# Attention of layer 0: scores in two passes from high and low parts, output written in parts, another order of units and modulation panels

## The chip, the core and the metric

The kernel runs on one core of a Trainium2 chip. The metric is the device time of one execution, in microseconds (us). Everything is fp32 data; the core's engines are TensorE (PE in the profile, matmuls), VectorE (DVE), ScalarE (ACT), GpSimd (POOL) and SyncE (SP, which issues most DMAs).

## The reference

Two transformer-like blocks of two layers each, on 512 tokens of width 1024 (and 256 context tokens in the first block). The change touches layer 0 of the first block, whose mixer is this:

```python
q, k, v = project(h)                        # 16 query heads, 4 key/value heads of 64
q, k = rope_2d(q, rows, cols), rope_2d(k, rows, cols)
qc, kc, vc = project(hc)                    # the same for the 256 context tokens
# tokens in 4 blocks of 128; each sees its own block, its neighbours (|distance| <= 128)
# and all 256 context tokens; a learned sink logit joins the softmax
s_win = einsum('bnqhgd,bnkhd->bnhgqk', qb, kw) * scale, masked
s_ctx = einsum('bnqhgd,blhd->bnhgql', qb, kc) * scale
p = softmax(concatenate([s_win, s_ctx, sinks]))
o = einsum(p_win, vw) + einsum(p_ctx, vc)
y = o.reshape(B, S, D_MODEL) @ w_o
# the context's own queries see only the 256 context tokens
```

Before and beside it, six modulation vectors (shifts, scales, gates) are made per layer by silu(c) @ ada_w + ada_b. A residual add, an MLP and then layer 1 and the second block follow; the change leaves them as they are.

## The kernel before

Every weight comes as a 1 MB "panel" (`sp_panels`, three buffers in a ring, issued by SP in the fixed order of `PANELS`). A projection is done to nearly fp32 accuracy from fp32r matmuls: `act_hi` (ScalarE) rounds a panel's half to fp32r, the high part, `dve_lo` (VectorE) subtracts to get the low part, the activations are split the same way, and `pe_tile` adds three matmuls per 128 rows of depth: high by high, low by high, high by low. Other matmuls take plain fp32 operands; the profile shows each of those as two records.

Each engine runs a program written out by hand, and its order is the order of the work. They meet only at semaphores (`wait_ge`, `then_inc`). Around the change the programs are, in time: modulation panels 0 to 7 and the first norm (`ada0_*`), queries, keys and values (`qkv_*`), attention (`att_*`), output projection (`wo_*` with the class `Proj`), MLP.

Attention works in 24 units: one group g (4 query heads that share a key head, 64 partitions) by one block of 128 queries. `AUNITS` lists them: 16 main units (query blocks 0 to 3, four groups each), then 8 context units. A main unit has 4 key blocks (query blocks 0 and 3) or 5 (1 and 2), a context unit 2. For unit n:

- scores: `att_pe.scores` writes one PSUM tile per head and key range (window, context), through banks 0 to 3 in turn; VectorE scales and masks the window tile into `S4` (L785), ScalarE copies the context tile (L743). Tile t waits until tile t-4 is read.
- maximum, negation (VectorE, L792 to L797); exp with sum (ScalarE, L750); the sink's term, reciprocal, four multiplications (VectorE, L803 to L810).
- output: per key block four transposes (L711), a copy to `PT` (ScalarE, L761), a matmul with the values into bank 6 (L719); VectorE copies the sum to `O` (L817).

TensorE's loop over n is: transpose of the last modulation row (`ada_tr`), scores of n, output of n-2, one modulation panel of 8 matmuls (`ada_mm`, L328), for the 16 panels 8 to 23 in the first 16 iterations. ScalarE's is: scores of n, `PT` copies of n-2, exps of n-1, copy of the modulation row. VectorE's is: `ada_add`, scores and maximum of n, copy of output n-2, softmax of n-1. After the loop all engines meet; `wo_act` and `wo_dve` split the first weights and all of `O` (L911, L921) into `OH` and `OL`, and then the 8x2 tiles of the output projection run (`Proj.pe`).

GpSimd does nothing in this stage.

Of the kernel before, what the change touches and what calls it, by code (L numbers as in the profile page):

```python
# [7 lines left out]
P = 128  # L8
# [148 lines left out]
def program(nc, ins, out_d, scratch):  # L157
# [115 lines left out]
    KT = alloc(stA, [P, 2, TT], name="kt")  # L273
    VT = alloc(stA, [P, 6, 256], name="v")
    QT = alloc(stA, [P, 8, TT], name="qt")
    CS = alloc(stA, [P, 2, T], name="cs")
    WM = alloc(stA, [P, 3, P], name="wm")

# [83 lines left out]
    class Norm:  # L362
        def __init__(self, name, st, src, hi, lo, segs, layer, which, banks, order):
            self.mm, self.ac, self.dv = sig(name + "_sum"), sig(name + "_act"), sig(name + "_dve")
            self.Q = [alloc(st, [P, T], name="nq") for _ in range(4)]
            self.A = alloc(st, [P, sum(g[1] for g in segs)], name="na")
# [95 lines left out]
    st2 = ExitStack()  # L462
# [3 lines left out]
    SQ = [alloc(st2, [P, T], name="sq") for _ in range(2)]  # L466
    QR = [alloc(st2, [P, T], name="qr") for _ in range(2)]
    RR = [alloc(st2, [P, T], name="rr") for _ in range(2)]
    VTMP = [alloc(st2, [P, T], name="vtmp") for _ in range(2)]
    st2.close()  # L470

# [117 lines left out]
    def qkv_act(e):  # L589
# [10 lines left out]
        for t, (m, s) in enumerate(QTILES):  # L600
# [15 lines left out]
        for t, (m, s) in enumerate(VTILES):  # L616
            n = BOTH[s][1]
            e.wait_ge(*qk_mm.at(*(("unit", QU + 10 + m) if s else ("vtile", t))))
            if t > 1:
                e.wait_ge(*qk_mm.at("vtr", t - 2))  # L620
            e.activation(VTMP[t % 2][:, 0:n], B[t % 4][:, 0:n], ACT.Copy).then_inc(*qk_ac.up("vcopy", t))

    def qkv_dve(e):
# [31 lines left out]
        for t, (m, s) in enumerate(VTILES):  # L655
# [3 lines left out]
                          B[4][:, 0:n].rearrange("p (a b) -> p a b", b=P)).then_inc(*qk_dv.up("v", t))  # L659

# [3 lines left out]
    O = alloc(stA, [P, 8, TT], name="o")  # L664
    st2 = ExitStack()
    S4 = [alloc(st2, [P, 4, 640], name="s4") for _ in range(3)]
    PT = [alloc(st2, [P, 5, 512], name="pt") for _ in range(2)]
    NSM = alloc(st2, [P, 3, 4, 8], name="nsm")
    st2.close()
    at_mm, at_ac, at_dv = sig("att_mm"), sig("att_act"), sig("att_dve")  # L670
    AUNITS = []
# [18 lines left out]
    def att_pe(e):  # L690
        def scores(n):
            g, q0, blocks, nw, mask = AUNITS[n]
            rows = slice(64 * (g % 2), 64 * (g % 2) + 64)
            for j, (i, i0, b0, cnt) in enumerate(ATILES[n]):
                t = ABASE[n] + j
                att_score_read(e, t - 4)
                e.matmul(B[t % 4][:, 0:cnt * P], QT[rows, 4 * (g // 2) + i, q0:q0 + P],  # L697
                         KT[rows, g // 2, b0 * P:(b0 + cnt) * P], start=True, stop=True).then_inc(*at_mm.up("score", t))

        def out(n):  # L700
# [4 lines left out]
            for j in range(nb + 2):  # L705
                if j < nb:
# [6 lines left out]
                    if j == nb - 1:  # L713
                        at_mm.also("s4", n)
                if j == 2 and n > 0:
                    e.wait_ge(*at_dv.at("o", n - 1))
                if j > 1:
                    e.wait_ge(*at_ac.at("pt", TBASE[n] + j - 2))
                    x = e.matmul(B[6][rows, :], VT[:, blocks[j - 2], 64 * g:64 * g + 64], PT[n % 2][:, j - 2, :],  # L719
# [4 lines left out]
        for n in range(NAU + 2):  # L724
            if 0 < n < 17:
                ada_tr(e, 7 + n)
            if n < NAU:
                scores(n)
            if n > 1:
                out(n - 2)  # L730
            if n < 16:
                ada_mm(e, 8 + n)

    def att_act(e):
# [20 lines left out]
        def out(n):  # L755
            for j in range(len(AUNITS[n][2])):
                t = TBASE[n] + j
                e.wait_ge(*at_mm.at("tr", t))
                if n > 1:
                    e.wait_ge(*at_mm.at("o", n - 2))  # L760
                e.activation(PT[n % 2][:, j, :], B[4 + t % 2][:, :], ACT.Copy).then_inc(*at_ac.up("pt", t))  # L761

        after(e, qk_mm, qk_dv)
        for n in range(NAU + 2):
            if n < NAU:
                scores(n)
            if n > 1:
# [3 lines left out]
            if n < 16:  # L771
                ada_row(e, 8 + n)

    def att_dve(e):
        def scores(n):
            g, q0, blocks, nw, mask = AUNITS[n]
            nb, s, sm = len(blocks), S4[n % 3], NSM[:, n % 3, :, :]
            for j, (i, i0, b0, cnt) in enumerate(ATILES[n]):
# [9 lines left out]
                at_dv.also("scores", n)  # L788
            if nw:
# [23 lines left out]
        def out(n):  # L813
            g, q0, blocks, nw, mask = AUNITS[n]
            rows = slice(64 * (g % 2), 64 * (g % 2) + 64)
            e.wait_ge(*at_mm.at("o", n))
            e.tensor_copy(O[rows, 4 * (g // 2):4 * (g // 2) + 4, q0:q0 + P],  # L817
                          B[6][rows, :].rearrange("p (a b) -> p a b", a=4)).then_inc(*at_dv.up("o", n))

        after(e, qk_mm, qk_dv)  # L820
        for n in range(NAU + 2):
            if 0 < n < 17:
                ada_add(e, 7 + n)
            if n < NAU:
                scores(n)
            if n > 1:
                out(n - 2)
            if 0 < n <= NAU:
                soft(n - 1)
# [3 lines left out]
    split_buffers("wo", stA)  # L833
    OH, OL = alloc(stA, [P, 8, TT], F32R, "oh"), alloc(stA, [P, 8, TT], F32R, "ol")
# [4 lines left out]
    class Proj:  # L839
# [12 lines left out]
        def waited(self, e, x):  # L852
            def part(k):
                e.wait_ge(*self.ready(k))
# [3 lines left out]
        def pe(self, e):  # L858
            ns = len(self.segs)
            for m in range(8):  # L860
                for s, sg in enumerate(self.segs):
# [4 lines left out]
                    if self.ready and t == 0:  # L866
                        x = self.waited(e, x)
# [38 lines left out]
    def wo_act(e):  # L906
        after(e, at_mm, at_dv)
        for u in range(2):
            act_hi(e, FIRST["wo"] + u)
        for k in range(8):  # L910
            e.activation(OH[:, k, :], O[:, k, :], ACT.Copy).then_inc(*wo_ac.up("hi", k))  # L911
        pj_wo.act(e)

    def wo_dve(e):
        after(e, at_mm, at_dv)
        e.wait_ge(*ad_dv.at(23))
        for u in range(2):
            dve_lo(e, FIRST["wo"] + u)
        for k in range(8):
            e.wait_ge(*wo_ac.at("hi", k))  # L920
# [2707 lines left out]
```

## Time and profile before

| | |
|---|---|
| median of 3 runs | 4224.87 us (4223.46 to 4234.95) |
| profiled execution | 4230.27 us, of it 4228.4 us span |
| PE busy | 3760.3 us, 89% |
| DVE, ACT, POOL busy | 2090.1, 1522.0, 161.9 us |
| attention, first score to last output copy | 203.3 to 508.1 us |
| first matmul of the output projection | 518.74 us |
| mean granted TensorE clock | 0.932 of full speed |

A row of the chain of waits is one link of the work that ended last, followed back from the end. A row by shape gives how many instructions of one line and shape there are, their busy time, the mean of one, and the idle time in front of them with what ended it. Each plain fp32 matmul counts twice, so "x64" of L697 are 32 matmuls. A matmul's length includes its way through the array; how fast they follow one another is read from their starts.

### The profile page before, as it was taken

To read this page: it belongs to the slowest core of one execution; us is meant where nothing else is said; L and a number is where in the kernel's file an instruction comes from. 1 tells how busy PE (TensorE), PEld (TensorE's weight loads), DVE (VectorE), ACT (ScalarE), POOL (GpSimd) and SP (SyncE) were. 2 spreads that over 40 slices of the span, in tenths; PEclk is the share of its full clock that TensorE was granted. 3 is DMA by queue.
4 is the path that set the end of the run, shared out by engine and by line. 5 is a ranking of instruction groups with operands and counts; after the bars stand their busy time and mean duration, and the time that the engine had idled before them with its cause. 6 is when DMAs were issued, how large, how long until landed. Compare 5 with 4: busy or idle time off the path is not lost.

```text
span 4228.4 us, 59602 instructions
## 1 busy us (share of the span) xinstructions
PE 3760.3 (89%) x24624; PEld 2879.9 (68%) x24624; DVE 2090.1 (49%) x3416; ACT 1522.0 (36%) x2724; POOL 161.9 (4%) x408
## 2 busy tenths in 40 slices
PE   7899799999977886888668999796999998889998
PEld 4744477778864566778537888575688866658886
DVE  4355443333456553666254455635444555544445
ACT  4345542222234552333143333333333243333333
POOL 0000000000000011333100000000000000000000
PEclk9999899999997987999889999795999999989999
DMA  4021013222112555565512222020122211112221
GB/s 181 30 80 60 31 60 120 110 110 80 70 63 76 158 138 154 151 158 142 156 40 80 90 100 108 31 76 22 70 90 100 100 68 50 50 55 89 101 90 60
DMA packets 295292, 380.56 MB, mean 90 GB/s; under 512 B 240496, under 2 KB 243440, under 8 KB 260336
## 3 DMA queue, kind: packets, MB, share of 16 engines
q1 hardware_dynamic: 281648, 330.88, 24.2%
q10 hardware_dynamic: 13376, 45.87, 2.9%
q8 instruction: 197, 3.23, 0.3%
q14 instruction: 71, 0.58, 0.0%
HBM read 331.61 MB, written 45.11 MB: 89 GB/s over the span
## 4 chain that ended last, share of the span: by engine, by line
PE 75%; DVE 10%; ACT 6%; DMA 3%; issue 2%; POOL 2%; SPq 1%; ACTq 0%; DVEq 0%; POOLq 0%
PE ps L254 18%; PE ps L255 17%; PE ps L256 17%; PE ps L328 4%; PE ps L719 2%; PE ps L697 2%; PE ps L1192 1%; PE ps L1194 1%; PE ps L1193 1%; PE ps L711 1%; DVE mx L1445 1%; DMA s_it<-rt 1%; ACT whi L239 1%; DVE xml L1450 1%; DVE wlo L246 1%
## 5 line engine op out<-in xcount | busy, mean ns | idle before, releaser
L246 DVE TENSOR_TENSOR wlo<-panel,whi 128x1024 fp32r<-128x1024 f32 (+1 forms) x524 | 503.6, 962 | 411.7 <-ACT whi L239 402.7
L239 ACT ACTIVATE whi<-panel 128x1024 fp32r<-128x1024 f32 (+1 forms) x524 | 442.1, 844 | 662.3 <-PE ps L256 627.5
L254 PE MATMUL ps<-xh,whi 128*128 128x512 f32 x1184 | 482.1, 407 | 34.7 <-DVE xl L2363 20.4
L254 PE MATMUL ps<-dh,whi 128*128 128x512 f32 (+1 forms) x1280 | 474.6, 371 | 0.0
L255 PE MATMUL ps<-dh,wlo 128*128 128x512 f32 (+1 forms) x1280 | 472.3, 369 | 0.0
L256 PE MATMUL ps<-dl,whi 128*128 128x512 f32 (+1 forms) x1280 | 470.5, 368 | 0.0
L255 PE MATMUL ps<-xh,wlo 128*128 128x512 f32 x1184 | 468.5, 396 | 0.0
L256 PE MATMUL ps<-xl,whi 128*128 128x512 f32 x1184 | 466.7, 394 | 0.0
L254 PE MATMUL ps<-hh,whi 128*128 128x512 f32 (+1 forms) x960 | 352.5, 367 | 26.3 <-DVE hl L448 26.2
L255 PE MATMUL ps<-hh,wlo 128*128 128x512 f32 (+1 forms) x960 | 339.9, 354 | 0.0
L256 PE MATMUL ps<-hl,whi 128*128 128x512 f32 (+1 forms) x960 | 339.1, 353 | 0.0
L254 PEld LDWEIGHTS ps<-xh,whi 128*128 128x128 f32 x1184 | 225.9, 191 | 103.5 <-issue 31.9
L1034 DVE TENSOR_TENSOR relu<-relu 128x512 f32<-128x512 f32 (+1 forms) x160 | 102.2, 638 | 370.0 <-ACT relu L1009 370.0
L254 PEld LDWEIGHTS ps<-dh,whi 128*128 128x128 f32 x1280 | 240.9, 188 | 48.7 <-issue 6.5
L256 PEld LDWEIGHTS ps<-dl,whi 128*128 128x128 f32 x1280 | 240.8, 188 | 41.2
L255 PEld LDWEIGHTS ps<-dh,wlo 128*128 128x128 f32 x1280 | 241.0, 188 | 40.1
L255 PEld LDWEIGHTS ps<-xh,wlo 128*128 128x128 f32 x1184 | 226.8, 192 | 49.7 <-issue 4.8
L256 PEld LDWEIGHTS ps<-xl,whi 128*128 128x128 f32 x1184 | 226.1, 191 | 49.7
L1009 ACT ACTIVATE relu<-ps 128x512 f32<-128x512 f32 (+1 forms) x160 | 88.7, 554 | 430.1 <-PE ps L256 425.0
L254 PEld LDWEIGHTS ps<-hh,whi 128*128 128x128 f32 x960 | 182.9, 190 | 69.4 <-issue 30.8
L255 PEld LDWEIGHTS ps<-hh,wlo 128*128 128x128 f32 x960 | 183.6, 191 | 27.8 <-issue 4.6
L1192 PE MATMUL ps<-xmh,whi 128*128 128x512 f32 (+1 forms) x368 | 149.0, 405 | 59.8 <-DVE xml L1450 59.6
(447 smaller groups left out, 5909.0 us busy)
## 6 DMA issues: line engine op xcount, KB each, us to landing
panel<-in_w SPq DMA_DIRECT2D x248, 1024.0 KB, 4.8
ld<-s_fe ACTq DMA_DIRECT2D x16, 1024.0 KB, 6.8
s_fe<-x SPq DMA_DIRECT2D x37, 256.0 KB, 2.8
ld<-s_fe ACTq DMA_DIRECT2D x24, 256.0 KB, 4.5
ld<-s_fe ACTq DMA_DIRECT2D x8, 768.0 KB, 6.6
vv<-s_fe ACTq DMA_DIRECT2D x24, 256.0 KB, 7.0
s_fe<-x SPq DMA_DIRECT2D x40, 128.0 KB, 2.2
s_ys<-yy SPq DMA_DIRECT2D x16, 256.0 KB, 2.9
```

The costliest lines, as they stand in the source:

```text
L239: e.activation(unit(u)[0][:, 0:kc, :], w, ACT.Copy).then_inc(*w_hi.up(u))
L246: e.tensor_tensor(lo[:, 0:kc, :], w, hi[:, 0:kc, :].bitcast(F32), SUB).then_inc(*w_lo.up(u))
L254: e.matmul(out, hi[:, k, :], xh, start=k == 0, stop=False)
L255: e.matmul(out, lo[:, k, :], xh, start=False, stop=False)
L256: last = e.matmul(out, hi[:, k, :], xl, start=False, stop=k == kc - 1)
L328: i = e.matmul(row, SC[:, k, :], w[:, k * 256:k * 256 + 256], start=k == 0, stop=k == 7)
L697: e.matmul(B[t % 4][:, 0:cnt * P], QT[rows, 4 * (g // 2) + i, q0:q0 + P], KT[rows, g // 2, b0 * P:(b0 + cnt) * P], start=True, stop=True). ...
L711: x = e.transpose(B[4 + t % 2][:, i * P:i * P + P], S4[n % 3][:, i, j * P:j * P + P], ID)
L719: x = e.matmul(B[6][rows, :], VT[:, blocks[j - 2], 64 * g:64 * g + 64], PT[n % 2][:, j - 2, :], start=j == 2, stop=j == nb + 1)
L1009: e.activation(r, B[t % 6][:, 0:n], ACT.Relu).then_inc(*self.ac.up("relu", f))
L1034: e.tensor_tensor(r, r, r, MUL).then_inc(*self.dv.up("sq", f))
L1192: e.matmul(out, hi[:, k, :], xh, start=k == 0, stop=False)
```

## The change

1. Memory: a new tensor `KW` holds all high and low parts; `KT` and the tables `CS` move, the norm's work tiles are shared with those of the projection, `VTMP` and two of the five `PT` tiles use `SG`. One wait is added for that: ScalarE's first query tile waits for the norm's last low part.
2. Keys: during the value tiles ScalarE rounds each group's keys into 64 partitions of `KX` and copies the result to the other 64 ("stacked"), and VectorE makes the low part `KL`.
3. Queries: per unit ScalarE rounds 64x512 into `QS` (`queries`), and GpSimd subtracts to put the low part into the other 64 partitions (`att_pool`).
4. Scores: instead of one plain fp32 matmul of depth 64 there are two fp32r matmuls: high and low queries, stacked to depth 128, by high keys; then high queries by low keys, depth 64.
5. Output: ScalarE rounds bank 6 into `OH` (`high`), VectorE then subtracts from bank 6 into `OL`; the splitting after the loop is gone, and so are the meeting of engines and the tensor `O`. The weight splits for the projection are done in the last two iterations. The projection's tiles of the first output row wait for `OL` of unit 22 (main) and 23 (context).
6. Order: the units come as main, main, context. Modulation panels 8 to 23 go to the second and third unit of each triple, and their matmuls stand inside the output, after the first two groups of transposes.
7. `PT` has one tile per key block instead of two sets; ScalarE does its exps ahead of the `PT` copies where a panel is done, and behind them elsewhere. VectorE's output step moves behind its softmax.

```diff
-    for qb in range(6):
-        blk = [b for b in (qb - 1, qb, qb + 1) if 0 <= b < 4] if qb < 4 else []
-        for g in range(4):
-            AUNITS.append((g, qb * P, blk + [4, 5], len(blk), 1 if qb == 0 else 0))
+    ASTEP = {n: 8 + n // 3 * 2 + n % 3 - 1 for n in range(24) if n % 3}
+    for n in range(24):
+        i = n // 3 * 2 + n % 3 if n % 3 < 2 else 16 + n // 3
+        qb, g = i // 4, i % 4
+        ...
@@ qkv_act
+            if t == 0:
+                e.wait_ge(*n0.dv.at("lo", *n0.steps[-1]))
...
+            if t < 2:
+                for g in (2 * t, 2 * t + 1):
+                    rows, other = HALF[g % 2], HALF[1 - g % 2]
+                    e.activation(KX[g % 2][rows, t, :], KT[rows, t, :], ACT.Copy).then_inc(*at_ac.up("kh", g))
+                    e.wait_ge(*at_ac.at("kh", g))
+                    e.activation(KX[g % 2][other, t, :], KX[g % 2][rows, t, :].bitcast(F32),
+                                 ACT.Copy).then_inc(*at_ac.up("kx", g))
+            if t == 2:
+                for n in range(2):
+                    queries(e, n)
@@ att_pe
+            e.wait_ge(*at_po.at("ql", n))
...
-                e.matmul(B[t % 4][:, 0:cnt * P], QT[rows, 4 * (g // 2) + i, q0:q0 + P],
-                         KT[rows, g // 2, b0 * P:(b0 + cnt) * P], start=True, stop=True).then_inc(*at_mm.up("score", t))
+                e.matmul(B[t % 4][:, 0:cnt * P], QS[n % 2][:, i, :], KX[g % 2][:, g // 2, keys], start=True, stop=False)
+                e.matmul(B[t % 4][:, 0:cnt * P], QS[n % 2][rows, i, :], KL[rows, g // 2, keys], start=False,
+                         stop=True).then_inc(*at_mm.up("score", t))
...
+                if j == 1 and n + 2 in ASTEP:
+                    ada_mm(e, ASTEP[n + 2])
                 if j == 2 and n > 0:
-                    e.wait_ge(*at_dv.at("o", n - 1))
+                    e.wait_ge(*at_dv.at("ol", n - 1))
@@ att_act
+            if 0 < n < NAU - 1:
+                queries(e, n + 1)
             if n < NAU:
                 scores(n)
-            if n > 1:
+            if n not in ASTEP and n > 1:
                 out(n - 2)
             if 0 < n <= NAU:
                 soft(n - 1)
+            if n >= NAU:
+                act_hi(e, FIRST["wo"] + n - NAU)
+            if n in ASTEP:
+                if n > 1:
+                    out(n - 2)
+                ada_row(e, ASTEP[n])
+            if n > 1:
+                high(n - 2)
@@ att_pool, new; called first in pool_program
+        for n in range(NAU):
+            e.wait_ge(*at_ac.at("qh", n))
+            e.tensor_tensor(QS[n % 2][other, :, :], QT[rows, 4 * (g // 2):4 * (g // 2) + 4, q0:q0 + P],
+                            QS[n % 2][rows, :, :].bitcast(F32), SUB).then_inc(*at_po.up("ql", n))
@@ att_dve
-            e.wait_ge(*at_mm.at("o", n))
-            e.tensor_copy(O[rows, 4 * (g // 2):4 * (g // 2) + 4, q0:q0 + P],
-                          B[6][rows, :].rearrange("p (a b) -> p a b", a=4)).then_inc(*at_dv.up("o", n))
+            e.wait_ge(*at_ac.at("oh", n))
+            e.tensor_tensor(OL[rows, heads, q0:q0 + P], B[6][rows, :].rearrange("p (a b) -> p a b", a=4),
+                            OH[rows, heads, q0:q0 + P].bitcast(F32), SUB).then_inc(*at_dv.up("ol", n))
@@ wo_act, wo_dve
-        after(e, at_mm, at_dv)
-        for u in range(2):
-            act_hi(e, FIRST["wo"] + u)
-        for k in range(8):
-            e.activation(OH[:, k, :], O[:, k, :], ACT.Copy).then_inc(*wo_ac.up("hi", k))
         pj_wo.act(e)
```

The order on TensorE, for one iteration in the middle of the attention. Before (scores of a main unit with 5 key blocks, output of another, a panel; `kt`, `qt` are keys and queries, `s` the probabilities, `cst` the identity):

```order
L697 MATMUL ps<-kt,qt 128x384
L697 MATMUL ps<-kt,qt 128x256
L711 MATMUL ps<-cst,s 128x128 x12
L719 MATMUL ps<-pt,v 64x512
L711 MATMUL ps<-cst,s 128x128 x4
L719 MATMUL ps<-pt,v 64x512
L711 MATMUL ps<-cst,s 128x128 x4
L719 MATMUL ps<-pt,v 64x512 x3
L328 MATMUL ps<-panel,silu 2x256 x8
L334 MATMUL ps<-cst,arow 128x2
L335 MATMUL ps<-cst,arow 128x2
```

After the change (third unit of a triple: the scores of a context unit, the output of a main unit; L743 and L744 are the two passes, L759 the transposes, L335 the panel, L769 the output):

```order
L743 MATMUL ps<-kw 128x256
L744 MATMUL ps<-kw 128x256
L341 MATMUL ps<-cst,arow 128x2
L342 MATMUL ps<-cst,arow 128x2
L759 MATMUL ps<-cst,s 128x128 x8
L335 MATMUL ps<-panel,silu 2x256 x8
L759 MATMUL ps<-cst,s 128x128 x4
L769 MATMUL ps<-pt,v 64x512
L759 MATMUL ps<-cst,s 128x128 x4
L769 MATMUL ps<-pt,v 64x512
```

The panel's matmuls moved from behind the output to between its second and third group of transposes, and the row's transposes from ahead of the scores to behind them.

ScalarE before, one iteration (scores, `PT` copies, exps, row copy):

```order
L743 ACTIVATE s<-ps 128x256 x4
L761 ACTIVATE pt<-ps 128x512 x5
L750 ACTIVATE s,nsm<-s,nsm 128x640 x4
L753 ACTIVATE nsm<-nsm 128x4
L341 ACTIVATE arow<-ps 2x256
```

ScalarE after, a second unit of a triple (here L661 is `queries`, L793 the context scores, L800 the exps, L811 the `PT` copies, L348 the row, L817 `high`):

```order
L661 ACTIVATE kw<-qt 64x512
L793 ACTIVATE s<-ps 128x256 x4
L800 ACTIVATE s,nsm<-s,nsm 128x640 x4
L803 ACTIVATE nsm<-nsm 128x4
L811 ACTIVATE pt<-ps 128x512 x2
L348 ACTIVATE arow<-ps 2x256
L817 ACTIVATE oh<-ps 64x4x128
```

Two instructions are new in each iteration, and the exps stand ahead of the `PT` copies.

## Rows read from the trace of the kernel before

**Rows 1.** By stretch: start:end, length, busy us (instructions) per engine, clock, DMA share, GB/s.
```profile
203.30:437.40 234.10, 223.16 (x929) 111.76 (x929) 124.05 (x248) 115.03 (x279) 0.00 (x0) 1.00 0.19 68
...
437.40:508.10 70.70, 55.98 (x208) 29.41 (x208) 33.83 (x98) 43.96 (x137) 0.00 (x0) 0.93 0.04 15
...
518.70:523.40 4.70, 4.66 (x11) 3.66 (x12) 1.12 (x1) 0.00 (x0) 0.00 (x0) 0.53 0.01 3
```

**Rows 2.** Chain of waits over one unit: start us, length us, engine, what.
```profile
311.05 4.50 PE ps L697 x16
...
317.49 1.00 PE ps L719 x2
...
318.49 0.59 PE ps L711 x4
...
320.67 2.72 PE ps L719 x6
...
323.39 3.56 PE ps L328 x16
...
326.97 0.38 ACT arow L341
...
327.68 4.50 PE ps L697 x16
```

**Rows 3.** TensorE in time, near the attention's end: start, length, idle before.
```profile
495.67 1.84 PE L711 MATMUL ps<-cst,s 128*128 128x128 f32 x8 [2.82 <-DVE s L810]
```

**Rows 4.** Chain of waits, from the last softmax to the output projection.
```profile
494.47 1.15 DVE s L810 x4
...
509.38 2.36 DVE wlo L246 x2
...
511.74 6.96 DVE ol L921 x8
...
518.74 0.79 PE ps L254
```

**Rows 5.** TensorE in time inside the output projection, two starts in a row.
```profile
543.01 0.28 PE L254 MATMUL ps<-oh,whi 128*128 128x256 f32 x1
...
543.12 0.28 PE L255 MATMUL ps<-oh,wlo 128*128 128x256 f32 x1
```

**Rows 6.** By shape, 203 to 508 us: count, busy us, mean ns, idle before.
```profile
L697 PE MATMUL ps<-kt,qt 64*128 64x384 f32 x64 | 26.6, 495 | 0.0
...
L743 ACT ACTIVATE s<-ps 128x256 f32<-128x256 f32 x96 | 35.3, 381 | 55.8 <-PE ps L697 55.4
...
L750 ACT ACTIVATE s<-s,nsm 128x640 f32<-128x640 f32 x32 | 26.0, 816 | 0.0
...
L750 ACT ACTIVATE s<-s,nsm 128x256 f32<-128x256 f32 x32 | 15.8, 500 | 0.0
...
L792 DVE TENSOR_REDUCE nsm<-s 128x4 f32<-128x2560 f32 x8 | 22.6, 2822 | 2.9 <-ACT s L743 2.9
...
L785 DVE SCALAR_TENSOR_TENSOR s<-ps,wm 128x384 f32<-128x384 f32 x32 | 17.8, 557 | 17.9 <-PE ps L697 17.9
...
L817 DVE COPY o<-ps 64x512 f32<-64x512 f32 x24 | 16.5, 689 | 82.2 <-PE ps L719 82.2
```

**Rows 7.** By shape, 46 to 600 us.
```profile
L621 ACT ACTIVATE vtmp<-ps 128x512 f32<-128x512 f32 x2 | 1.2, 597 | 13.2 <-PE ps L256 13.2
...
L911 ACT ACTIVATE oh<-o 128x768 fp32r<-128x768 f32 x8 | 6.0, 827 | 0.0
...
L921 DVE TENSOR_TENSOR ol<-o,oh 128x768 fp32r<-128x768 f32 x8 | 7.0, 948 | 0.0
```

**Rows 8.** All engines in time, end of the norm and first query tile.
```profile
70.68 0.76 DVE L448 TENSOR_TENSOR hl<-nq,hh 128x256 fp32r<-128x256 f32 x2 [0.38 <-ACT hh L428]
...
71.81 0.57 ACT L612 ACTIVATE qr<-ps 128x512 f32<-128x512 f32 x1
```

**Rows 9.** By shape, GpSimd, whole span.
```profile
L1537 POOL TENSOR_TENSOR x<-x 128x512 f32<-128x512 f32 x5 | 5.2, 1039 | 1465.5 <-DVE x L1514 1465.5
```

More of the change, by code:

```diff
@@ L272, in program @@
     stA = ExitStack()
-    KT = alloc(stA, [P, 2, TT], name="kt")
     VT = alloc(stA, [P, 6, 256], name="v")
     QT = alloc(stA, [P, 8, TT], name="qt")
-    CS = alloc(stA, [P, 2, T], name="cs")
     WM = alloc(stA, [P, 3, P], name="wm")
+    KW = alloc(stA, [P, 44, P], F32R, "kw")
+    KX = [KW[:, 12 * i:12 * i + 12, :].rearrange("p (a b) c -> p a (b c)", a=2) for i in range(2)]
+    KL = KW[:, 24:36, :].rearrange("p (a b) c -> p a (b c)", a=2)
+    QS = [KW[:, 36 + 4 * i:40 + 4 * i, :] for i in range(2)]
+    st2 = ExitStack()
+    CS = alloc(st2, [P, 2, T], name="cs")
     def start_act(e):
@@ L365, in __init__ @@
             self.Q = [alloc(st, [P, T], name="nq") for _ in range(4)]
-            self.A = alloc(st, [P, sum(g[1] for g in segs)], name="na")
+            self.A = alloc(st, [P, T * len(segs)], name="na")
             self.src, self.hi, self.lo, self.segs = src, hi, lo, segs
@@ L621, in qkv_act, with queries @@
             e.activation(VTMP[t % 2][:, 0:n], B[t % 4][:, 0:n], ACT.Copy).then_inc(*qk_ac.up("vcopy", t))
+            if t == 0:
+                e.wait_ge(*qk_dv.at("out", 18))
+            if t < 2:
[8 more added lines that the diff above has]
+                    queries(e, n)
+    def queries(e, n):
+        g, q0 = AUNITS[n][0], AUNITS[n][1]
+        rows = HALF[g % 2]
+        if n > 1:
+            e.wait_ge(*at_mm.at("scores", n - 2))
+        e.activation(QS[n % 2][rows, :, :], QT[rows, 4 * (g // 2):4 * (g // 2) + 4, q0:q0 + P],
+                     ACT.Copy).then_inc(*at_ac.up("qh", n))
     def qkv_dve(e):
@@ L714, in out @@
                         at_mm.also("s4", n)
+                if j == 1 and n + 2 in ASTEP:
+                    ada_mm(e, ASTEP[n + 2])
                 if j == 2 and n > 0:
-                    e.wait_ge(*at_dv.at("o", n - 1))
+                    e.wait_ge(*at_dv.at("ol", n - 1))
                 if j > 1:
                     e.wait_ge(*at_ac.at("pt", TBASE[n] + j - 2))
-                    x = e.matmul(B[6][rows, :], VT[:, blocks[j - 2], 64 * g:64 * g + 64], PT[n % 2][:, j - 2, :],
+                    x = e.matmul(B[6][rows, :], VT[:, blocks[j - 2], 64 * g:64 * g + 64], PT[j - 2][:, :],
                                  start=j == 2, stop=j == nb + 1)
@@ L788, in scores, with maxima @@
                 at_dv.also("scores", n)
+        def maxima(n):
+            g, q0, blocks, nw, mask = AUNITS[n]
+            nb, s, sm = len(blocks), S4[n % 3], NSM[:, n % 3, :, :]
             if nw:
@@ L850, in key, with waited @@
             return ("unit", self.u0 + m) if s == len(self.segs) - 1 else ("tile", m, s)
-        def waited(self, e, x):
+        def waited(self, e, s, x):
             def part(k):
-                e.wait_ge(*self.ready(k))
+                e.wait_ge(*self.ready(s, k))
                 return x(k)
@@ L865, in pe @@
                     x = self.src(sg)
-                    if self.ready and t == 0:
-                        x = self.waited(e, x)
+                    if self.ready and m == 0:
+                        x = self.waited(e, s, x)
                     pe_tile(e, self.u0 + m, B[t % 6][:, 0:sg[1]], x).then_inc(*self.mm.up(*self.key(m, s)))
@@ L906, in wo_act @@
     def wo_act(e):
-        after(e, at_mm, at_dv)
-        for u in range(2):
-            act_hi(e, FIRST["wo"] + u)
-        for k in range(8):
-            e.activation(OH[:, k, :], O[:, k, :], ACT.Copy).then_inc(*wo_ac.up("hi", k))
         pj_wo.act(e)
     def wo_dve(e):
-        after(e, at_mm, at_dv)
         e.wait_ge(*ad_dv.at(23))
[L917 to L920, printed above, removed]
-            e.tensor_tensor(OL[:, k, :], O[:, k, :], OH[:, k, :].bitcast(F32), SUB).then_inc(*wo_dv.up("lo", k))
         pj_wo.dve(e)
     def wo_pe(e):
-        e.wait_ge(*wo_dv.at("lo", 7))
         pj_wo.pe(e)
@@ L3379, in pool_program @@
     def pool_program(e):
+        att_pool(e)
         feat_pool(e)
```

86 lines of the change are left out of this document (56 added, 30 removed).

## The prediction

> **What bounds the kernel now.** I read the busy table by stretches first, since the change touches one stage. The reader should see two regimes [rows 1]: from 203.3 to 437.4 us TensorE is busy 223 of 234 us at full clock, while VectorE and ScalarE are busy about half; from 437.4 to 508.1, the last context units, it is busy only 56 of 70.7 at a mean clock of 0.93. Then the chain of waits over one unit [rows 2]: it stays on TensorE nearly throughout. A unit with 5 key blocks takes 16.6 us (score start 311.05, next one 327.68): scores 4.5, output 7.84 (from their end at 315.55 to 323.39), panel 3.56, and some 0.7 us in which TensorE waits for the copy of the modulation row (0.38) and turns it. Inside the output a block costs 0.59 for its transposes and 1.00 for its matmul. At the end TensorE waits for the softmax multiplications, up to 2.82 us [rows 3], and from 508.1 on it has nothing at all: weights and output are split on the other engines, 8 subtractions take 6.96 us, and the projection starts at 518.74 [rows 4], at a clock of 0.53 for its first 4.7 us [rows 1]. So TensorE work comes off one for one in the first regime, until another engine is later than TensorE.
>
> **Scores.** A matmul with 384 key columns is two records of 495 ns [rows 6]; with four 384s and four 256s the scores take the 4.5 us of the chain. The fp32r matmuls of the projection start 0.11 to 0.12 us apart at 256 columns [rows 5]; by columns that is 0.17 at 384. Two passes of four such pairs are 2.3 us. That is the floor. It isn't reached, because four banks hold eight tiles, so tile 4 waits until VectorE has read tile 0. Before, VectorE read while TensorE was still slow (17.9 us of idle waiting for TensorE [rows 6]). Now it comes late: at the start of an iteration it first has to finish the output of the unit before, and this is a relay of ScalarE's rounding of bank 6 (0.60, the copy of the same size [rows 7]) and then VectorE's subtraction (0.69, as its copy now [rows 6]). With 0.1 for the handover VectorE starts reading 1.4 us after TensorE starts scoring. Reads take 0.557 each [rows 6]. Tile 4 can start at 2.0, tile 6 at 2.55, the last tile ends at 3.2. ScalarE is behind it as well: rounding 0.6, next queries 0.5 to 0.6, then four reads of 0.38 [rows 6]; it ends at 3.7.
>
> **One triple of iterations**, main units of 5 blocks (iteration n scores unit n and outputs unit n-2; the row's transposes are 0.3):
>
> First (scores a main unit, outputs a main one, no panel): 3.2 + 0.3 + 7.84 = 11.35. ScalarE makes the last PT copy at 9.3 and only then the exps of the context unit, four at 0.50 [rows 6], with sink term 11.6; VectorE's reciprocal and multiplications (1.15 [rows 4]) end at 13.2 and the subtraction of the output at 13.9. That is 2.55 after TensorE began the next scores, not 1.4.
>
> Second (scores main, outputs a context unit, panel): reads start at 2.55, so tile 4 at 3.1, tile 6 at 3.7, end 4.3. Row, 8 transposes, panel: 0.3 + 1.1 + 3.56 = 9.3. ScalarE starts the main unit's exps at 4.9, four at 0.82 [rows 6], 8.2. Its sink exp needs VectorE, which is in the maximum until 8.1 (2.82 from 5.2 on [rows 6]): 8.9. First PT copy done at 9.55. Two output matmuls of 0.9 (2.72 / 3) end at 11.3.
>
> Third (scores context, outputs main, panel): the four tiles find four free banks, 0.95. Row and 8 transposes 2.4, panel 6.0. ScalarE's reads end at 2.75, exps and sink 6.35, first PT copy 6.95; TensorE waits 0.95. Then three blocks of 1.59, less the last matmul, and 2.72 for the last three matmuls, the same 6.5 as from the third transposes on now: 13.5.
>
> Sum 36.2. With 4 blocks two outputs are shorter by 1.59 each, reads and exps shorter by a few tenths each: 31.5. There are four triples of each: 4 x 36.2 + 4 x 31.5 = 270.8. The first two iterations output nothing (-9.1), but the start waits for its first softmax (+0.9). The two iterations behind the loop: output 6.5, then the wait for the last softmax, to 8.45 (ScalarE can start those exps only at 4.5), the first weight subtraction (1.2 of the 2.36 [rows 4]) stands ahead of output 22's on VectorE, so bank 6 is free at 10.3; the last matmul ends at 12.1. Attention then takes 270.8 - 9.1 + 0.9 + 12.1 = 274.7 us.
>
> **The end.** The projection starts right behind it: its first weights are split by 9.6, its main input is ready at 10.3, and the context's is needed 5.5 us later. So 203.3 + 274.7 = 478.0 in place of 518.74, 40.7 us earlier. The stretch of 4.7 us at clock 0.53 would be 2.2 shorter at full speed. Waits of 2.0 and 0.8 us stand just ahead, and after one of 2.82 eight transposes took 1.84 [rows 3] in place of twice 0.59; so I take 1.3. Sum: 42 us.
>
> **Costed at nothing.** Key split: ScalarE does two groups per value tile, four copies of 0.83 each as for `oh` [rows 7], 3.3 us; it idles 13.2 us before two of these tiles [rows 7], 6.6 each. VectorE's `KL` is 0.95 twice [rows 7], beside the same tiles. Without this cover it would be 6.6 us. The shared norm tiles: the last low part is done at 70.68 + 0.76 = 71.44 and ScalarE's first query tile starts at 71.81 [rows 8], so the added wait costs nothing, and 0.4 at most if both slip. SP: a panel is released in the same order as before, an iteration of 10 us or more ahead of its use, with the DMA busy 0.19 [rows 1]; the order of the queue doesn't change. GpSimd's subtraction is new here: 1.04 for 128x512 elsewhere [rows 9]. It starts when the queries are rounded, 1.3 into an iteration, and is needed at the next one's start, 9.5 or more: 7 us to spare. Bounds: zero, or, if each held up the scores for its full length, 24 x 1.04 = 25 us. I take zero, as the time to spare is seven times its length.
>
> Here the Trainium skill speaks against the change (SBUF — State Buffer, section on the two separate sides): VectorE in its two-port mode, or with two SBUF inputs, and GpSimd take one shared port pair as an exclusive lock for a whole instruction. No run here shows both at work in this stage. By that rule only the first iteration of a triple has an overlap, since GpSimd starts at about 12.7 while VectorE multiplies until 13.2; VectorE's reads from PSUM aren't concerned. The delay would be up to 1 us in each of 8 triples, and the sum 34 in place of 42.
>
> **Forecast.** 4230.3 (profiled, with 1.9 around the span) - 42 = 4188.3. The median of the runs is 5.4 lower than the profiled one, so 4183.
>
> **Rivals.**
> *The relay costs nothing and TensorE sets the pace throughout.* For it: both other engines are half idle [rows 1]. Then first, second and third iterations are 0.9, 2.3 and 0.95 shorter, 4.1 per triple, 33 in all; gain 75, 4150. Against: VectorE's program order puts the output behind the softmax. Chance 0.13.
> *ScalarE sets the pace.* It gets 24 x (0.55 + 0.6) = 28 us more, now in a chain of ten waits per iteration; at 1 us more in each iteration (0.1 per handover, or GpSimd held by the port) the gain is 42 - 24 = 18, 4207. Chance 0.17.
> *Slower: the 64-row strided copies.* `queries`, `high` and the subtraction each move 64x512 in a [4,128] pattern on half of the lanes and into the fp32r type. If each took double (0.6, 0.6, 0.7 more) and the two of the relay also delayed softmax, every iteration is 1.9 to 2.2 longer; it turns over at 42 / 24 = 1.75, and at 2.2 the time is 4183 + 53 = 4236. Against: the present copy of just this pattern takes 0.689 [rows 6]. Chance 0.03.
> *It doesn't do what it says:* the two passes run no faster than the plain matmul (depth 64 and 128 mixed). Then main scores stay at 4.5 where I have 3.2 and 4.3, context scores at 1.9 where I have 0.95: 1.3 + 0.2 + 0.95 per triple, 8 times, is 20; gain 22, 4203. Chance 0.05.
>
> The forecast itself has 0.62, with its own range 4172 to 4194 (half a microsecond per iteration either way). The range for 8 in 10 goes towards both neighbours: 4157 to 4204. What a measurement can tell from no change is 0.3%, 12.7 us. Faster by more than that (gain above 12.7): 0.94; within: 0.03; slower: 0.03.
>
> **What the profile after would show.** Right: score matmuls start 0.11 to 0.17 us apart in the first four tiles, then idle until VectorE's read; main scores 3 to 4.5 us long, context scores 1; the chain passing through `oh` and `ol` and the exps; the first matmul of the projection at about 478; no idle of TensorE for `kw` of GpSimd. Wrong: TensorE idle for GpSimd's part, chain rows of ScalarE longer than 3 us per iteration, the first score later than 203.3, or a clock clearly under 1.00 between 210 and 465, which by the first 4.7 us of the projection would cost nearly double for each microsecond spent there.

## The result, and the profile after

| | before | after |
|---|---|---|
| median of 5 runs each, one chip | 4234.35 us (4223.46 to 4234.95) | 4258.6 us (4251.22 to 4261.79) |
| ratio after to before | | 1.0063, 95% interval 1.0045 to 1.0082 |
| profiled execution, span | 4230.27, 4228.4 us | 4253.16, 4251.4 us |
| first matmul of the output projection | 518.74 us | 546.04 us |
| time at half clock from 203 us to there | 19.7 us | 95.5 us |

The change makes the kernel 0.63% slower; 4183 had been predicted, and the range ended at 4204. All of it arises in the attention: the first scores begin at 203.6 (before 203.3), and the projection starts 27.3 us later than before. "Time at half clock" is worked out from the granted clock of one-microsecond stretches: where it reads 0.5 the whole microsecond counts, where it reads 0.9 a fifth of it. Before, 9.2 of the 19.7 us lie behind 509.5, where TensorE has nothing to do until the projection; after, TensorE is at work in all 95.5.

The 4183 was the median of the first three of the five runs before, less 42; the median of all five, less the same 42, would give 4192. The sign and the miss stay the same.

By stretch, after (start:end, length, busy us and instructions of PE, PEld, DVE, ACT, POOL, clock, DMA share, GB/s), against [rows 1]:

```profile
203.30:437.40 234.10, 231.74 (x764) 110.75 (x764) 111.19 (x236) 124.66 (x309) 20.78 (x16) 0.85 0.13 46
437.40:508.10 70.70, 70.26 (x250) 34.23 (x248) 30.53 (x75) 40.65 (x101) 7.46 (x6) 0.90 0.16 59
...
364.10:368.60 4.50, 4.50 (x15) 2.43 (x14) 2.26 (x4) 2.28 (x5) 1.26 (x1) 1.00 0.00 0
368.60:375.30 6.70, 6.70 (x21) 3.73 (x20) 3.94 (x6) 2.27 (x5) 0.00 (x0) 0.50 0.00 0
```

TensorE is busier than before (231.74 against 223.16 of 234.10), gets through fewer instructions (764 against 929), and its mean clock is 0.85 where it was 1.00. The last two rows are one such fall: 4.5 us of scores at full clock, and right behind them 6.7 us at half, with TensorE busy in every microsecond of both.

The chain of waits over one unit, after (start, length, engine, what), against [rows 2]:

```profile
318.71 0.37 PE ps L743
319.09 0.37 PE ps L744
319.46 0.31 PE ps L743
319.77 0.31 PE ps L744
...
324.19 0.15 PE ps L341
```

L743 is the first pass (depth 128), L744 the second (depth 64). The scores of a main unit with 5 key blocks take 324.19 - 318.71 = 5.5 us; before 4.5, predicted 3.2 and 4.3. Here the chain stays on TensorE: it doesn't go through `oh` and `ol`, as it would if the relay bound.

The same passes by shape, 203 to 545 us (count, busy us, mean ns, idle before), against [rows 6]:

```profile
L744 PE MATMUL ps<-kw 64*128 64x256 f32 x128 | 54.5, 426 | 0.0
L743 PE MATMUL ps<-kw 128*128 128x256 f32 x128 | 54.3, 424 | 1.8 <-DVE s L858 1.3 <-DVE v L699 0.5
...
L744 PE MATMUL ps<-kw 64*128 64x384 f32 x32 | 14.9, 467 | 0.0
L743 PE MATMUL ps<-kw 128*128 128x384 f32 x32 | 14.6, 455 | 1.4 <-DVE s L858 1.4
```

TensorE waits 2.7 us in all for VectorE's reads (1.3 and 1.4). So nothing that I had put in the way of the fast passes held them up; they are slow by themselves. The end of the attention, chain of waits, against [rows 3, 4]:

```profile
539.45 1.14 DVE s L887 x4
540.59 1.13 DVE wlo L246
541.75 0.70 DVE ol L895
542.50 3.54 PE ps L769 x4
546.04 0.47 PE ps L254
546.51 0.24 PE ps L255
```

The tail has the predicted order: last subtraction, last output matmuls (two, of two records each), then the projection, 0.24 us from matmul to matmul. The output matmuls stand at half clock and take 3.54 us. The only row of GpSimd in the attention, against [rows 9]:

```profile
L845 POOL TENSOR_TENSOR kw<-qt,kw 64x512 fp32r<-64x512 f32 x22 | 28.6, 1299 | 276.9 <-ACT kw L661 276.9
```

### The profile page after: what moved, and what is told of

Its sections match the earlier page's. It is cut to its first block, busy times and chain, and to the rows that moved or that the text cites. A ratio compares the mean times of both kernels' runs of the same rounds, so it can differ in the third digit from the quotient of the medians.

```text
span 4251.4 us, 59708 instructions
## 1 busy us (share of the span) xinstructions
PE 3803.9 (89%) x24624; PEld 2889.0 (68%) x24624; DVE 2085.4 (49%) x3412; ACT 1551.2 (36%) x2772; POOL 193.5 (5%) x432
## 4 chain that ended last, share of the span: by engine, by line
PE 73%; DVE 9%; ACT 6%; DMA 4%; POOL 3%; issue 2%; SPq 2%; ACTq 0%; DVEq 0%; POOLq 0%
PE ps L254 17%; PE ps L255 17%; PE ps L256 17%; PE ps L335 4%; PE ps L769 2%; PE ps L759 1%; DMA s_it<-rt 1%; PE ps L744 1%; PE ps L743 1%; PE ps L1263 1%; POOL ri L2132 1%; POOL tp L2129 1%; PE ps L1265 1%; PE ps L1264 1%; DVE mx L1516 1%
## 5 line engine op out<-in xcount | busy, mean ns | idle before, releaser
L246 DVE TENSOR_TENSOR wlo<-panel,whi 128x512 fp32r<-128x512 f32 (+1 forms) x519 | 497.9, 961 | 410.1 <-ACT whi L239 400.3
L239 ACT ACTIVATE whi<-panel 128x512 fp32r<-128x512 f32 (+1 forms) x519 | 436.9, 842 | 637.4 <-PE ps L256 605.2
```

Of the source, the lines that this page charges most:

```text
L239: e.activation(unit(u)[0][:, 0:kc, :], w, ACT.Copy).then_inc(*w_hi.up(u))
L246: e.tensor_tensor(lo[:, 0:kc, :], w, hi[:, 0:kc, :].bitcast(F32), SUB).then_inc(*w_lo.up(u))
```

## The experiments

Theory A: passes of depth 128 and 64 alternate, each change costs time at the array, and the clock falls with it. Rival B: the new order of the units or the place of the panels does it. Rival C: the relay around the scores does it. "Before" was run again beside each group: 4230.8 (11 runs, experiments 1 to 4), 4228.4 (13, 5 to 8), 4230.2 (7, 9 to 11) and 4232.2 us (7, the last one); ratios are to that, with 95% intervals.

**Both passes at depth 128.** The second pass multiplies all 128 rows. Low queries then also meet the low keys of the neighbour group, a small product that isn't in the reference; so it is in every kernel below with both passes at depth 128.

```diff
- e.wait_ge(*at_dv.at("kl", g))
+ e.wait_ge(*at_dv.at("kl", g | 1))
- e.matmul(..., QS[n % 2][rows, i, :], KL[rows, g // 2, keys], start=False,
+ e.matmul(..., QS[n % 2][:, i, :], KL[:, g // 2, keys], start=False,
```

> The second pass takes all 128 partitions of the queries and of the low keys (the other 64 hold the low keys of the group's neighbour, times the low queries, a product about as small as the one left out anyway), so that both passes have depth 128. Theory A (a change of depth between two matmuls keeps the second's weights from being loaded beside the first, some 0.2 us for each of 320 changes, and the thin stream behind it lowers the granted clock): passes of 256 columns start 0.12 us apart and not 0.31, main scores last 3 to 4.5 us and not 5.5, mean clock of the attention stage about 0.98 and not 0.86, time 4180 to 4200. Theory B (two fp32r matmuls with new weights each cost 0.3 us whatever their depth): starts stay 0.31 to 0.37 apart, 4255. Theory C (the spacing is from depth, but the clock falls for the new order of the units and the waits in it): starts 0.12 apart, clock still near 0.87, time 4225 to 4240.

Measured: 4176.57 us, ratio 0.9867 (0.9846 to 0.9887), 3 us below theory A's range; projection from 473.6; 10.2 us at half clock. Its TensorE in time (start, length, what, idle before), and then its chain of waits at the same place:

```profile
302.13 0.28 PE L743 MATMUL ps<-kw 128*128 128x256 f32 x1
302.25 0.28 PE L744 MATMUL ps<-kw 128*128 128x256 f32 x1
302.37 0.34 PE L743 MATMUL ps<-kw 128*128 128x384 f32 x1
302.55 0.34 PE L744 MATMUL ps<-kw 128*128 128x384 f32 x1
302.72 0.28 PE L743 MATMUL ps<-kw 128*128 128x256 f32 x1
302.84 0.28 PE L744 MATMUL ps<-kw 128*128 128x256 f32 x1
304.83 0.44 PE L743 MATMUL ps<-kw 128*128 128x384 f32 x1 [1.71 <-DVE s L858]
```

```profile
303.11 0.35 DVE s L887
303.49 0.69 DVE ol L895
304.21 0.57 DVE s L858
304.78 0.04 issue
304.83 0.44 PE ps L743
```

The same number of passes with the same columns now start 0.12 and 0.18 us apart, where the mixed ones take 0.31 and 0.37. That is 0.19 less at both widths. And here, at last, is the picture that the prediction drew: four tiles at once, then a wait of 1.71 us behind softmax, `ol` and the first read. The rows that one matmul reads are worth 82 us.

The weight loads (PEld) show where the time goes. In the changed kernel each load starts together with its own matmul, in all 320 passes:

```profile
364.10 0.19 PEld L743 LDWEIGHTS ps<-kw 128*128 128x128 f32 x1 [0.81 <-issue]
364.10 0.44 PE L743 MATMUL ps<-kw 128*128 128x384 f32 x1
364.47 0.18 PEld L744 LDWEIGHTS ps<-kw 64*128 64x128 f32 x1 [0.19 <-issue]
364.47 0.44 PE L744 MATMUL ps<-kw 64*128 64x384 f32 x1
```

With one depth a load starts with the matmul before its own. The loads for the passes that start at 302.25 and 302.37 above:

```profile
302.14 0.19 PEld L744 LDWEIGHTS ps<-kw 128*128 128x128 f32 x1
302.25 0.19 PEld L743 LDWEIGHTS ps<-kw 128*128 128x128 f32 x1
```

**Both passes at depth 64.** The first pass leaves out low queries by high keys.

```diff
- e.matmul(..., QS[n % 2][:, i, :], KX[g % 2][:, g // 2, keys], start=True, ...
+ e.matmul(..., QS[n % 2][rows, i, :], KX[g % 2][rows, g // 2, keys], start=True, ...
```

> The first pass takes only the 64 partitions with the high parts (the product of low queries and high keys is left out), so that both passes have depth 64. Theory A (the change of depth): starts 0.12 to 0.17 us apart as in e1, time near e1's if the clock goes by how closely matmuls follow, and not by their depth. Theory B: starts 0.31 to 0.37 apart, 4255. If the clock goes by how much of the array works, the clock stays low here (0.86 to 0.9) with starts close, and the time is 4210 to 4240.

Measured: 4189.08 us, ratio 0.9896 (0.9873 to 0.9918); projection from 486.9; 44.4 us at half clock. The passes start 0.12 and 0.18 us apart, as in the first experiment. So it is the change of depth and not depth 128 or 64 by itself. The projection starts 13.3 us later than there, with 34.2 us more at half clock; why the clock is lower, with the same distances inside the scores, is open.

**Four first passes, then four second ones.**

```diff
- for j, (i, i0, b0, cnt) in enumerate(ATILES[n]):       # both passes of a tile
+ for j0 in range(0, len(ATILES[n]), 4):
+     four = list(enumerate(ATILES[n]))[j0:j0 + 4]
+     for j, (i, i0, b0, cnt) in four:  ...              # first pass, depth 128
+     for j, (i, i0, b0, cnt) in four:  ...              # second pass, depth 64
```

> The first passes of four tiles stand in a row and then their four second passes, so the depth changes 4 times in a main unit instead of 16. Theory A: 12 of 16 changes at 0.2 us go, 2.4 us per main unit and 1.2 per context unit, 45 us at full clock in all, less what the reads by VectorE take back since the first tile is whole only after five matmuls; time 4195 to 4225. Theory B: no change, 4255 or more, since the reads start later.

Measured: 4190.49 us, ratio 0.9899 (0.9879 to 0.992), 5 us below theory A's range; projection from 490.2; 37.5 us at half clock. The work is the same as in the changed kernel to the last column. Its TensorE in time (L744 is its first pass, L748 its second; each row merges four passes, two of 384 and two of 256 columns, and names the first one's shape):

```profile
299.87 0.85 PE L744 MATMUL ps<-kw 128*128 128x384 f32 x4
300.65 0.84 PE L748 MATMUL ps<-kw 64*128 64x384 f32 x4
301.81 1.02 PE L744 MATMUL ps<-kw 128*128 128x384 f32 x4 [0.31 <-DVE s L862]
302.76 0.84 PE L748 MATMUL ps<-kw 64*128 64x384 f32 x4
```

Four passes that take 4 x 0.34 = 1.4 us when mixed take 0.8. A single change costs as much as each of the many: the pass behind it starts 0.21 us after its neighbour in place of 0.12, and the next one 0.28 in place of 0.18. Of the 320 weight loads 227 start ahead of their matmul; the other 89 are the first of each group of four, 80 of them, and 9 behind a wait.

By the count of changes of depth between the two passes, the one on leaving the scores included:

| changes | kernel | projection from | at half clock | median |
|---|---|---|---|---|
| 0 | both at depth 128 | 473.6 | 10.2 us | 4176.6 us |
| 80 | four by four | 490.2 | 37.5 us | 4190.5 us |
| 320 | the changed kernel | 546.0 | 95.5 us | 4258.6 us |

By the start of the projection all 320 cost 72.4 us. 320 x 0.19 is 61; the slow passes also fill 19 us in which TensorE would wait (25.5 us idle in the first experiment's attention, 19.0 of it before a first pass; 6.1 and 3.2 in the changed kernel). The rest, some 30, goes with 85.3 us more at half clock. For the 80 the same account is 15, less 6 filled, and 27.3 us more at half clock; measured 16.6. So some 7 of these 16.6 go with the clock. That the medians differ by 13.9, close to 80 x 0.19, is chance in part.

**Plain fp32 scores**, the key split gone, everything else kept.

```diff
- e.matmul(B[t % 4][:, 0:cnt * P], QS[n % 2][:, i, :], KX[g % 2]..., start=True, stop=False)
- e.matmul(B[t % 4][:, 0:cnt * P], QS[n % 2][rows, i, :], KL[rows, ...], start=False, stop=True)
+ e.matmul(B[t % 4][:, 0:cnt * P], QT[rows, 4 * (g // 2) + i, q0:q0 + P], KT[rows, g // 2, keys], ...)
```

> The changed kernel with the scores as one plain fp32 matmul again, from the unsplit queries and keys; the key split is gone, the splitting of the queries by ScalarE and GpSimd, the new order, the output in parts and the panels inside the output stay. Theory A (the two passes are what costs): main scores 3.65 to 4.5 us instead of 5.5 to 5.8, clock 0.97 or more, time 4190 to 4210. Theory C (the order and the relay of the output are what costs): clock still under 0.9, time 4240 to 4260.

Measured: 4214.87 us, ratio 0.9959 (0.9944 to 0.9974), 5 us above theory A's range. Everything but the two passes is together a gain of 16 us; with the passes as written the kernel is 44 us slower than this.

**The old order of the units**, once with both passes at depth 128, once with the change as it is, once with plain scores.

```diff
- ASTEP = {n: 8 + n // 3 * 2 + n % 3 - 1 for n in range(24) if n % 3}
+ ASTEP = {n: 7 + n for n in range(1, 17)}
- i = n // 3 * 2 + n % 3 if n % 3 < 2 else 16 + n // 3
+ i = n
```

> e1 (both passes at depth 128) with the units in the old order, 16 main ones and then 8 context ones, and panels 8 to 23 in iterations 1 to 16; the panel's matmuls stay inside the output. If the new order is worth what the prediction gave it (context units spread out so that the end doesn't wait for their softmax), the last eight units take about 6 us each with TensorE idle 1 us or more in each, and the time is 4190 to 4205. If the order is worth nothing, 4177.

> The changed kernel as it is (depth 128, then 64), only with the units in the old order and panels in iterations 1 to 16. If the fall of the clock comes from the thin stream of the mixed passes, it stays: 80 us or more at half clock, time 4250 to 4275. If it needs the new order as well, under 50 us at half clock, and 4220 to 4240.

> e4 (plain fp32 scores) with the units in the old order: what is left of the change is the output in parts, the query splitting, the panels inside the output and the exps ahead of the copies. If the new order made the clock fall in e4 (44 us at half clock, one dip per triple), the dips go and the time is near e4's 4215 or 5 to 10 us lower. If the relay of the output makes the dips, they stay, and it is 4215 to 4230.

Measured: 4178.29 us (0.988, 0.9858 to 0.9902), 4262.23 us (1.0078, 1.0055 to 1.01) and 4200.32 us (0.9928, 0.9908 to 0.9949). With the new order: 4176.6, 4258.6, 4214.9. So the new order is worth 2 and 4 us, about nothing, with two passes of either kind, and costs 15 with plain scores: B falls, as far as the order goes. The low clock of the mixed passes doesn't need the new order either: 119.5 us at half clock in the old one, in its slowest run (4269.5). With plain scores in the new order the clock dips once in each triple, 44.3 us at half clock against 22 in the old one. Why is open. So mixed passes aren't the only thing here that lowers the clock.

**Panel behind the output**, with both passes at depth 128; ScalarE's row copy follows the high parts.

```diff
- if j == 1 and n + 2 in ASTEP: ada_mm(e, ASTEP[n + 2])     # inside out(n)
+ if n > 1 and n in ASTEP: ada_mm(e, ASTEP[n])              # behind out(n - 2)
```

> e1 with the panel's matmuls behind the output again, and the copy of its row behind the output's rounding. The prediction says that the panel inside the output covers ScalarE's exps ahead of the first copies: without it TensorE waits up to 3 us there in 16 of 24 iterations, 4195 to 4220. If it covered nothing, 4177.

Measured: 4239.72 us, ratio 1.002 (1.0008 to 1.0032), 63 us above the first experiment and 20 above the expected range. By shape, 203 to 540 us:

```profile
L767 PE MATMUL ps<-pt,v 128*64 128x512 f32 x128 | 83.0, 761 | 25.9 <-ACT pt L811 25.1 <-DVE ol L896 0.8
...
L759 PE MATMUL ps<-cst,s 128*128 128x128 f32 x352 | 55.4, 294 | 29.5 <-ACT pt L811 27.8 <-DVE s L888 1.6
```

TensorE waits 52.9 us for ScalarE's `PT` copies (4.0 in the first experiment), and 54.7 us are at half clock (10.2 there); the expectation had counted the wait alone. In iterations with a panel the changed program puts the exps ahead of those copies; a panel inside the output covers that, and one behind it doesn't. The last experiment tells the two apart.

**The relay out of the way**, both passes at depth 128: ScalarE's queries behind its score reads, VectorE's output of n-3 behind the reads of n; then the same in the old order.

```diff
+ scores(n)                       # ScalarE
  if 0 < n < NAU - 1: queries(e, n + 1)
- scores(n)
  scores(n)                       # VectorE
+ if 2 < n <= NAU: out(n - 3)
...
- if n > 1: out(n - 2)
+ if n >= NAU: out(n - 2)
```

> Both passes at depth 128 (as in the first experiment), and the relay of the query parts out of the way of the scores: ScalarE computes the queries of unit n+1 behind the scores of unit n and not ahead of them, VectorE scales the output of unit n-3 behind the score reads and not ahead of them. The sum of the prediction says that a triple then waits some 2.9 us less (0.7 in the first iteration, 1.9 in the second, 0.3 in the third), eight times: the output projection starts at about 451 instead of 473.6 and the time is about 4155 us. Theory 'VectorE's score reads and the relay ahead of them bound the attention now': 4150 to 4162. Rival 'TensorE's own stream bounds it, the waits are filled otherwise': 4174 to 4180, and the idle time of TensorE for VectorE's reads (19 us there) shows up elsewhere. Rival on the other side 'the output, scaled later, holds the buffer of the next output matmul': over 4185.

> The same as the run before, with the units in the old order (the eight context units last) and the panels of the modulation at iterations 1 to 16. Theory 'the order is worth nothing once the passes have one depth': within 4 us of the run before (with the relay in its old place the two orders differed by 1.7 us). Rival 'interleaving pays only when the relay does not bound': 10 us or more above it, since eight context units in a row then run at the pace of their exps while the main units carry two panels each.

Measured: 4166.84 us (0.985, 0.9827 to 0.9872), projection from 465.8, and 4169.89 us (0.9856, 0.983 to 0.9883). The first is a gain of 9.7 where some 22 were expected, so neither theory's number; the second lies 3 us above it, as expected if the order is worth nothing. By shape, 203 to 465 us:

```profile
L769 PE MATMUL ps<-pt,v 128*64 128x512 f32 x128 | 66.3, 621 | 5.1 <-ACT pt L811 4.3 <-DVE ol L895 0.8
...
L759 PE MATMUL ps<-cst,s 128*128 128x128 f32 x352 | 52.1, 282 | 7.8 <-ACT pt L811 4.9 <-DVE s L887 2.9
L743 PE MATMUL ps<-kw 128*128 128x256 f32 x128 | 35.1, 300 | 5.9 <-DVE s L858 5.4 <-DVE v L699 0.5
...
L743 PE MATMUL ps<-kw 128*128 128x384 f32 x32 | 12.5, 390 | 3.4 <-DVE s L858 3.4
```

The idle time before the first pass falls from 19.0 to 9.3 us, and that before transposes and output matmuls rises from 6.5 to 12.9: two thirds of the wait moved to `PT` copies and softmax. The projection starts 7.8 us earlier, of which that leaves 3.3; the time at half clock falls from 10.2 to 2.9 us. This is the fastest kernel of the study, 1.5% faster than before. C is a second-order effect: it shows here, with fast passes, while in the changed kernel TensorE waits only 2.7 us for the reads.

**Plain scores, old order, panel behind the output**: the diff of the eighth experiment on the seventh.

> Plain fp32 scores and the old order, as in the seventh experiment (4200 us), with the panel of the modulation behind the output instead of inside it, and the row copied behind the high parts: what is left of the change is the output in parts and the smaller edits. Theory 'the place of the panel carries the gain of that run': back to the kernel before, 4224 to 4236. Rival 'the output's parts carry it': 4200 to 4208. Half of each: about 4215.

Measured: 4275.8 us, ratio 1.0106 (1.008 to 1.0131). Outside both theories: 75 us above the seventh and 46 above the kernel before. TensorE is idle 49.1 us for the copies, and 75.0 us are at half clock, in 18 stretches. The expectation had overlooked ScalarE's order.

**Copies ahead of the exps**, on the eighth experiment.

```diff
- if n not in ASTEP and n > 1:
+ if n > 1:
      out(n - 2)
  if 0 < n <= NAU: soft(n - 1)
- if n in ASTEP and n > 1:
-     out(n - 2)
```

> The eighth experiment (both passes at depth 128, panel behind the output, row behind the high parts: 4239.7 us), with one thing more put back as before: ScalarE copies the transposed tiles ahead of the exps in every iteration, also in those with a panel. There TensorE was idle 52.9 us for those copies (4 us in the first experiment, where the panel lies inside the output and covers the exps). Theory 'the panel inside the output pays because it covers exps that were put ahead of the copies, and by its place alone it is worth little': about 4185 to 4195, near the first experiment's 4176.6. Rival 'the panel inside the output pays whatever ScalarE's order': 4225 or more.

Measured: 4178.56 us, ratio 0.9888 (0.9865 to 0.9911), 6 us below the expected range and near the first experiment, as its theory says. By shape, 203 to 478 us:

```profile
L767 PE MATMUL ps<-pt,v 128*64 128x512 f32 x128 | 66.5, 623 | 2.6 <-ACT pt L811 1.7 <-DVE ol L893 0.8
...
L759 PE MATMUL ps<-cst,s 128*128 128x128 f32 x352 | 53.5, 287 | 6.9 <-ACT pt L811 4.0 <-DVE s L885 2.9
```

The 52.9 us shrink to 5.7. Panel inside with exps first, and panel behind with copies first, differ by 2 us; panel behind with exps first is worse than both, by 61 to 63 us. The fourth combination, panel inside with copies first, was not run, so what the place is worth with copies first isn't shown.

## Why the prediction was wrong

The step that failed is "Two passes of four such pairs are 2.3 us. That is the floor." It was priced from [rows 5], where neighbouring fp32r matmuls have one depth. In the change they don't, and each change of depth adds 0.19 us: a pass goes from 0.12 to 0.31 at 256 columns and from 0.18 to 0.37 at 384, and its weights are loaded at its own start and no longer beside the pass before. The experiments show that this is the mechanism: same work, grouped by four, 68 us faster. A second step failed with it: the sum has the whole attention at full clock, and 95.5 us of it ran at half.

The Trainium skill (TensorEngine Tiling (Array Packing), Key Properties) says "Mode switching requires drain"; its section Available Configurations lists 128 and 64 rows as different modes. The prediction named the mix in its last rival but didn't weigh this rule. The page writes of packing several tiles into the array, and whether a lone matmul of depth 64 counts as such a mode it doesn't say. The runs agree with the rule if it does; it gives no duration, the traces say 0.19 us.

With the measured passes put into the prediction's own triple, the scores of 5.5, 5.5 and 2.5 in place of 3.2, 4.3 and 0.95 add 2.3 + 1.2 + 1.55 = 5.05 a triple, some 40 us in eight (in four of them, with 4 key blocks, roughly so). The projection would then start at 518.4 in place of 478.0, as late as before. The clock comes on top, and since the sum was made at full clock, all 95.5 us count. At half clock an output matmul pair takes 1.90 in place of 1.00, but a pass 0.51 in place of 0.31 and 12 transposes 2.85 in place of 1.77, so a microsecond there contains 0.38 to 0.47 of loss: 36 to 45 us in all, an estimate. That gives 555 to 563; measured is 546.0, 9 to 17 us less. Most of that is known: the wait of 0.95 us for the first `PT` copy that the prediction has in each third iteration, 7.6 us, is gone (TensorE waits 0.5 us for these copies in the whole attention), and the prediction was too long in the first experiment too, by 4.4 us though 10.2 were at half clock. The projection starts 27.3 us later than before, and the time is 24 us longer. That the alternating passes cause the low clock is shown, since only they differ between the first experiment and the changed kernel. What in them the clock answers to is not, and the low clock of the second, fourth, eighth and eleventh experiments has no cause shown.

Point by point:
- *Two passes no faster than plain* (rival, 0.05, 4203): the right cause, at a quarter of its price (20 us above the forecast where it was 76). I let the mixed passes cost what the plain ones cost; they cost 1.0 us more a main unit, 0.6 more a context unit, and the clock.
- *The clock*: taken as full, from [rows 1]. The sign named for "wrong", a clock clearly under 1.00 between 210 and 465, is there (0.85). No rival had a clock that the change itself lowers, and so none came out over 4236.
- *The relay, the reads, the triple*: right, as the first experiment shows, where the passes have the predicted distance. There, from 301.67 to 336.8, a second, a third and a first iteration took 11.1, 12.6 and 11.4 us (predicted 11.3, 13.5, 11.35); projection from 473.6 (predicted 478.0), time 4176.6 (predicted 4183). That the total came so near is luck in part: the third iteration is 0.9 us shorter than predicted, and 10.2 us at half clock, which the sum didn't have, go the other way.
- *The end*: right in kind, the projection follows the last output matmul, and its first matmuls run at full clock.
- *Costed at nothing*: key split and shared tiles show no cost beyond 0.3 us (first scores at 203.6). GpSimd took 1.30 on average instead of 1.04, and TensorE never waited for it. The lock of the shared port that the prediction weighed, with up to 8 us, shows in no wait of TensorE.
- *Slower by strided copies* (rival): false. The three take 0.63 (`queries`), 0.59 (`high`) and 0.69 us (the subtraction).
- The chance of 0.03 for slower was far too small. It covered one mishap of my own making, not the operation whose price had no row in the trace: alternating depth.

## What to carry to other kernels

Price a matmul from a row in which its neighbours are of the same kind as in the new code: next to one of another depth it cost 0.19 us more, above its own 0.12. Group matmuls by depth, or pad the smaller one to full depth with operands that exist anyway. After a change to what TensorE issues read the granted clock at once, since here it cost some 30 us more on top of the gaps. And when one of two interlocking orders is moved (here exps ahead of copies, panel inside output), look at what the other one covered.

## What the hardware did that I had not expected

- Going from depth 128 to 64 or back costs 0.19 us, the same at 256 and at 384 columns; around it the weight load (0.18 to 0.19 us) starts with its own matmul, where with one depth it starts 0.12 to 0.18 us earlier.
- The clock fell to half while the records had TensorE busy for 100% of the time (364.10 to 375.30 above). In the first experiment it stayed full through scores in which TensorE was busy only 2.59 of 4.30 us (same columns as above); so in these rows the busy share doesn't foretell the clock:

```profile
301.70:306.00 4.30, 2.59 (x17) 2.39 (x16) 3.73 (x10) 2.32 (x7) 1.37 (x1) 1.00 0.00 0
```

- At half clock transposes and passes don't take twice as long: 0.24 for 0.15 us, and 0.51 for 0.31.
- GpSimd's subtraction over 64x512 took 1.30 us on average, longer than the 1.04 for 128x512 elsewhere. Half of the partitions was no saving here, though the two differ in more than that: this one writes fp32r, and into the other 64 partitions.
